# TensorE's level loop of the delta-rule recurrence, its head set at slot 106 of an instruction block

## What is computed

```python
def step(state, inp):
    r_t, w_t, k_t, v_t, kk_t, a_t = inp
    sa = jnp.einsum('bhvk,bhk->bhv', state, -kk_t)
    state = (state * w_t[:, :, None, :]
             + sa[..., None] * (kk_t * a_t)[:, :, None, :]
             + v_t[..., None] * k_t[:, :, None, :])
    y = jnp.einsum('bhvk,bhk->bhv', state, r_t)
    return state, y
_, y = lax.scan(step, state0, xs)
```

## Time and profile before

| | us |
|---|---|
| median of 3 runs | 2882.18 |
| lowest and highest run | 2873.37, 2884.86 |
| the profiled execution's own time | 2869.96 |
| its span, first to last instruction | 2868.2 |
| TensorE matmuls busy | 2747.3 (96% of the span) |
| VectorE busy | 1956.5 (68%) |
| ScalarE busy | 1357.8 (47%) |
| GpSimd busy | 1428.0 (50%) |

### The profile page before, as it was taken

How to read it: one execution, slowest core, us unless ns; L and a number is a source line. 1 busy time by engine, 2 the same in 40 slices (tenths; PEclk the granted TensorE clock), 3 DMA queues, 4 the chain that set the end, 5 groups by cost and what they waited for, 6 DMA issues and landing times.

```text
span 2868.2 us, 62975 instructions
## 1 busy us (share of the span) xinstructions
PE 2747.3 (96%) x25488; PEld 2181.6 (76%) x25488; DVE 1956.5 (68%) x2854; ACT 1357.8 (47%) x2348; POOL 1428.0 (50%) x961
## 2 busy tenths in 40 slices
PE   8899899999999999998999999899899999999998
PEld 6444566887888888876678878888788788888887
DVE  6687887788777787788132347677648766656667
ACT  5476977234344333346442246566414543334445
POOL 0001000333776767774446636676542676677772
PEclk9899999999999999999999999999999999999999
DMA  9100000622232322331442411222312112111111
GB/s 320 59 1 16 1 2 1 237 87 66 89 96 75 101 73 88 95 110 30 160 149 88 156 68 55 88 75 70 115 30 59 44 59 59 44 56 47 59 44 74
DMA packets 194407, 225.43 MB, mean 79 GB/s; under 512 B 14863, under 2 KB 151650, under 8 KB 194210
## 3 DMA queue, kind: packets, MB, share of 16 engines
q1 hardware_dynamic: 182529, 180.66, 20.1%
q10 hardware_dynamic: 11680, 42.01, 4.0%
HBM read 185.15 MB, written 37.22 MB: 78 GB/s over the span
## 4 chain that ended last, share of the span: by engine, by line
PE 69%; DVE 10%; ACT 4%; issue 4%; POOL 3%; DMA 1%; ACTq 0%; DVEq 0%; SPq 0%; POOLq 0%
PE ps L149 18%; PE ps L150 18%; PE ps L151 18%; DVE uc L1091 2%; PE ps L2305 2%; PE ps L2294 1%; PE ps L3802 1%; PE ps L2316 1%; PE ps L3885 1%; PE ps L3879 1%; PE ps L3891 1%; ACT d_r L2447 1%; PE ps L3862 1%; DVE d_r L2707 1%; POOL w_lo L739 1%
## 5 line engine op out<-in xcount | busy, mean ns | idle before, releaser
L149 PE MATMUL ps<-x_hi,w_hi 128*128 128x512 f32 x1160 | 453.3, 391 | 2.9 <-POOL w_lo L739 2.9
L151 PE MATMUL ps<-x_hi,w_lo 128*128 128x512 f32 x1160 | 451.5, 389 | 0.0
L150 PE MATMUL ps<-x_lo,w_hi 128*128 128x512 f32 x1160 | 451.4, 389 | 0.0
L739 POOL TENSOR_TENSOR w_lo<-w_room,w_hi 128x512 fp32r<-128x512 f32 x188 | 288.3, 1545 | 235.0 <-ACT w_hi L1253 235.0
L739 POOL TENSOR_TENSOR w_lo<-sq_room,w_hi 128x512 fp32r<-128x512 f32 x182 | 285.0, 1577 | 220.0 <-ACT w_hi L1253 220.0
L1091 DVE SCALAR_TENSOR_TENSOR uc<-u,pc,uc 128x1024 f32<-128x1024 f32 x176 | 326.9, 1868 | 26.4 <-ACT uc L1267 15.6
L1079 DVE TENSOR_TENSOR u<-u,ps 128x512 f32<-128x512 f32 x228 | 151.2, 684 | 194.6 <-PE ps L151 170.1
L149 PE MATMUL ps<-g_hi,w_hi 128*128 128x512 f32 x640 | 251.5, 393 | 6.7 <-DVE h L1157 6.5
L149 PEld LDWEIGHTS ps<-x_hi,w_hi 128*128 128x128 f32 x1160 | 217.7, 188 | 50.6 <-POOL w_lo L739 5.8
L151 PEld LDWEIGHTS ps<-x_hi,w_lo 128*128 128x128 f32 x1160 | 217.7, 188 | 45.7
L150 PEld LDWEIGHTS ps<-x_lo,w_hi 128*128 128x128 f32 x1160 | 217.8, 188 | 44.7
(11 more groups left out here) (492 smaller groups left out, 6767.9 us busy)
## 6 DMA issues: line engine op xcount, KB each, us to landing
w_room<-in_f_w_up_dram SPq DMA_DIRECT2D x48, 512.0 KB, 5.1
rwkv_scratch<-rp_stage ACTq DMA_DIRECT2D x48, 512.0 KB, 3.5
sq_room<-in_f_w_up_dram SPq DMA_DIRECT2D x40, 512.0 KB, 4.8
ada_w<-in_ada_w_dram SPq DMA_DIRECT2D x80, 256.0 KB, 2.7
rc_raw<-rwkv_scratch SPq DMA_DIRECT2D x28, 512.0 KB, 3.7
d_ada_w<-in_ada_w_dram SPq DMA_DIRECT2D x24, 512.0 KB, 8.7
d_r<-in_ada_w_dram ACTq DMA_DIRECT2D x24, 512.0 KB, 5.7
sq_room<-in_f_w_down_dram SPq DMA_DIRECT2D x24, 512.0 KB, 4.2
```

The costliest lines, as they stand in the source:

```text
L149: pe.matmul(out, w_hi, x_hi, start=first, stop=False, skip_group_check=skip)
L150: pe.matmul(out, w_hi, x_lo, start=False, stop=False, skip_group_check=skip)
L151: return pe.matmul(out, w_lo, x_hi, start=False, stop=last, skip_group_check=skip)
L739: pool.tensor_tensor(slot_of(k.w_lo, s), src, slot_of(k.w_hi, s).bitcast(F32), ALU.subtract).then_inc(w_lo_done, 1)
```

## The change

```diff
@@ -4178,6 +4178,8 @@
+    FETCH_BLOCK, HEAD_SLOT = 256, 106
+
     def pe_all(pe):
@@ -4204,6 +4206,7 @@
             banks_opened(pe, p)
             first_z(pe, p)
+            pe.addr_align(FETCH_BLOCK, offset=HEAD_SLOT - 1, max_nops=0)
             with pe.Fori(1, LV[-1]) as lv:
                 level_pe(pe, p, lv)
             last_u(pe, p)
```

## The result

The changed kernel takes 2886.59 us (median of 8 runs, 2877.25 to 2895.91), the kernel before 2874.05 us (median of 8, 2869.6 to 2884.86). The ratio is 1.0042, 95% interval 1.0027 to 1.0057: slower by 12 us, within the half percent that the prediction took as its bound. The direction is the forecast's; its size (+19 us) and its time (2900 us) are too high, by 6.5 and 13 us.

What follows compares the result with a forecast made beforehand. TensorE, 69% of the chain setting the end, was taken to wait for instruction blocks in loops' first turns. Terms 16.8 + 3.9 - 1.4 = +19 us on 2882 gave 2901, stated as 2900; range 2890 to 2907, 8 in 10 2866 to 2914.

Steps and rivals of the forecast that it cites:

- head wait: At the loop's head in pairs 1 to 7, TensorE waits about 1.3 to 1.6 us for its block.
- second stop: In pairs 1 to 7, 150 instructions behind the head, TensorE waits about 2.5 us for the next block.
- fetched anew: Rival: the loop-head branch discards the packet under way and asks again, +13 us on top, 2913 us; chance 0.08.
- back edges: Rival about the loop's branches back, counted with the faster outcomes; its description is cut from the text; chance 0.02.
- The first rival: Loops of pairs 1 to 7 run like pair 6 since both blocks come in time: -14 us, 2868; chance 0.14.
- the others: Remaining rivals: no effect, 2882 us (0.12); branch asks for its block anew, 2913 us (0.08); back edges (0.02).
- the distance of the two packets: In pairs 1 to 7, the second block's packet starts 4.2 us after the first's, between 3.4 and 4.6.
- the lead of the first: The first packet starts before the head would run: 0.8 us in pairs 2 to 6, 1.5 in 1, 0.5 in 7.
- the falls of the clock: In three of pairs 4 to 7, two close gaps bring a clock fall: +3.9 us, bounds 0 and +6.0.
- The straight code: Code outside the loops shifts, its small stops may come or go: counted at nothing, within 2 us either way.
- Pair 7's stop behind its loop: The 1.45 us stop behind pair 7's loop goes, as a block boundary falls elsewhere: -1.4 us.
- the base: Starting time of the kernel before: profiled 2870 us plus 12 us to the median of runs, 2882 us.

Runs made afterwards that it cites:

- the second time: The changed kernel, unaltered, run and profiled again: 2886.37 us, ratio 1.0031 against the kernel before.
- slot 20: As the changed kernel, but loop heads set at slot 20 instead of 106: 2891.53 us, ratio 1.0059 against the kernel before.
- the levels written out: Kernel before with the loop's four levels written out four times, no loop and no directive on TensorE: 2941.73 us, ratio 1.0232.
- slot 180: As the changed kernel, but loop heads set at slot 180 instead of 106: 2896.45 us, ratio 1.0064 against the kernel before.
- at the pair's start: Kernel before plus a directive at the start of pairs 1 to 7 asking for slot 0, none at loop heads: 2893.55 us, ratio 1.0068.

## Why the prediction was right or wrong

**What held.** The mechanism: a head wait and a second stop, on the line foretold (L3885), in every pair from 1 to 7; 146 packets for "about 147"; nothing fetched anew by the branch; no block fetched again by a later turn, which would have made dozens of packets more, so no cost of back edges; the later use of a block 2.2 to 2.8 us behind its packet, for 2.4. The head waits of 1.1 to 1.5 us (1.2 to 1.65 the second time) in pairs 1 to 6 are what was named, 1.3 to 1.6. That is in part luck: the packet had 0.6 us more lead than I put in pairs 2 to 6, which alone would have made 1.0 us of wait, but the branch ended 2.3 to 2.8 us behind it. The second stop, 1.0 to 1.75 us, was not the 2.5 that was named. The first rival's slot was right and its jump wrong; the others fell: the directive is obeyed, and no head gap is 3 us.

What failed is the pricing of three terms: the distance of the two packets (4.2 us, measured 3.3), the lead of the first (0.8 us, measured 1.4) and the falls of the clock (+3.9 us, measured -4.0 and -2.2).

**The distance of the packets, 4.2 us, was wrong.** It measured 3.0 to 3.6 us, mean 3.3, in the seven pairs of each of the two profiles. I took 4.2 from pair 2, where TensorE walks into the block: it stands 0.45 us for it, until 1789.2, and the next packet starts 1.8 us behind that. At the jump the next packet starts 0.5 to 0.8 us behind the head, and the distance is the same with the head at slot 20 (3.0 to 3.6 us). So it goes with the jump and not with the slot; why the next packet comes sooner behind a jump isn't shown. No row of before shows that state; the shortest distance there, 3.4 us in pair 0, came nearest, and I used it only as an end of the range. First packet to first branch was to be 8.8 us; it is 7.4 to 9.0, mean 8.2 (8.5 the second time).

**The lead a of the first packet** was 0.8 us for pairs 2 to 6; it is 1.4 to 1.5 us (0.95 to 1.4 the second time). In pairs 1 and 7 it is 1.4 and 0.4 (1.2 and 0.6), near the 1.5 and 0.5 named. From where the head would have run to the first branch this makes 6.3, 6.9, 6.0, 7.3, 6.5, 6.3 and 8.6 us in pairs 1 to 7, against 7.3, 8.0 five times, and 8.3. Set against before, the term is +9.5 us instead of +16.8 (+12.9 in the second profile). Over the seven pairs of the first profile the distance makes -6.3 us of that error and the lead -3.0, while the way from the second packet to the first branch, 4.9 us instead of 4.6, gives 1.8 back.

**The clock: +3.9 us was wrong in sign.** No run shows that term; what the runs show in its place is -4.0 and -2.2 us. In the first profile of the changed kernel the granted clock falls to 0.50 in three pairs (2, 4, 7), as it did before in three (1, 2, 3; pair 2 in the earlier trace rows); in the second it falls in all seven. A stretch of pair 2 in the first:

```profile
1797.80:1801.20 3.40, 3.19 (x119) 3.19 (x121) 0.85 (x2) 1.75 (x4) 0.64 (x1) 0.50 0.02 5
```

The first turn's branch is at 1800.8 us, near its end. Before, the low stretch began 0.8 to 1.4 us behind the end of a stop and lay in the second turn, which rose from 3.7 to between 4.8 and 5.1 us. Now it lies mostly over the rest of the first turn (two falls of the second profile, in pairs 2 and 7, reach into the second turn, 4.8 and 4.6 us), where it costs 0.5 to 0.9 us (pairs 1, 3, 5: 5.2, 5.0, 5.1 us without, 5.7, 5.8, 5.8 with). Turns two to four sum to 79.7 us over pairs 1 to 7 (81.5 in the second profile), against 83.7 in both of before: -4.0 and -2.2 us, where I had put +3.9. I had counted falls, three more, and priced each at 1.1 to 1.5 us, from three later turns of 12.6 to 13.0 us with a fall before against 11.5 in pair 4 without; the cost of the falls in first turns is inside the +9.5 and +12.9. Why a fall costs less there isn't shown: TensorE was busy for 3.19 of the 3.40 us, so it is not that the low clock lies over a stop. Falls come and go in the kernel before too, in pairs 1, 2 and 7 in its second profile, with the same 83.7.

**The straight code** I set at nothing, within 2 us either way; it is +4.3 us, about the four stops at L3845, and +2.2 with two of them the second time. **Pair 7's stop behind its loop** did go, but other boundaries took its place: the straight code behind it is 115.8 us for 115.0, and -1.4 was +0.8. It is counted in the +4.3.

**The sum.** 9.5 - 4.0 + 4.3 = 9.8, with 0.5 us left over, for the 10.3 in the trace; 12.9 - 2.2 + 2.2 = 12.9 for 13.2 in the second. The forecast was 16.8 + 3.9 - 1.4 = 19. The other 8 us of the error in the time are the base: I stood on 2882, the middle of three runs from 2873 to 2885, while 8 runs give 2874 and later ones 2876.

**Boundaries and blocks.** Boundaries do stop TensorE with these 64x64 products: 1.5 to 2.4 us at single ones before, 70 us in all with the levels written out. And blocks are not fetched twice in the loops: the number of packets leaves no room for it, with bodies over three blocks (slot 180: 147 packets) as well, and while the feed-forward's loop of 1157 instructions turned, TensorE's queue had no packet.

## What to carry to other kernels

Code that is executed once at the pace of these 64x64 products waited for its blocks (70 us of stops with the levels written out), so look where a loop's head lies before paying to move it, and don't move it by a jump: a branch into a block that isn't there stopped the engine for 1 to 4.5 us, more than the better slot gave back (at the pair's start 24.7 us of branches for 12.4 in the loops), and shifting the straight code mostly moved the stops (-4.7 us in the loops, +5.3 in the straight code). Where a term is a distance between two events, take it from a row in the same state (here: the engine standing still), and where there is none, build it from its parts. Ask in which stretch a low clock will lie before pricing its falls, and take the base from more than three runs where a few microseconds matter.

## What the runs showed of the hardware

- A taken branch into a block that isn't there lasts as long as the wait: 1.1 to 2.5 us at slot 106, 2.2 to 3.5 at slot 20, 2.9 to 4.5 at a pair's start. In these four profiles (slot 106 has two) it ended 2.3 to 2.9 us behind the start of the target's packet, also where that started after the branch had begun. It lasts 0.18 us where the target is in the same block (pair 0 at slot 106), 0.31 where the next block is already there (slot 180).
- Blocks of 16 KB came as single packets: 3.0 to 3.6 us apart around the jump to slot 106 or 20 (pairs 1 to 7), 3.3 at the shortest and 4.1 in the median where code is walked (the levels written out). The changed kernel's second stops in pairs 1 to 7 ended 2.2 to 2.8 us after the packet's start.
- Filler instructions on TensorE, recorded at 13 ns, pass at some 74 ns each (229 in 17.0 us).
- The granted clock fell to 0.50 for 3.4 us (at times 6.8) after stops of 1 to 2.5 us, not after each and not in every execution of the same code: with the changed kernel in three pairs once, in seven another time.
- The same loop at the same slot differs by up to 2.5 us from one execution to the next (pair 2: 18.9, 19.0 and 16.4 us; pair 3: 19.1, 16.7 and 19.2).
